# A hybrid decoder block on one core: expert keys turned by block transposes on VectorE, one equality for both gate masks, and 78 instead of 64 early blocks

## Chip, cores and metric

One Trainium2 chip, one of its cores. The metric is the device time in microseconds (us) of one execution. Lower is better.

## What is computed

One layer: adaLN conditioning, sliding-window attention and a gated delta rule in parallel, a gated mix of the two with an output projection, then a PEER channel mixer. 512 tokens, width 1024, everything in float32. The change is in the output projection, in PEER and in what connects them:

```
mix = (sigmoid(gate_a) * y_a + sigmoid(gate_b) * y_b) @ w_out
x = x + gate1 * mix
h2 = rms_norm(x, norm2_gain) * (1.0 + scale2) + shift2
x = x + gate2 * peer(h2, peer_w_q, peer_sub_keys, peer_u, peer_v)

# peer: 8 heads, 2 x 128 sub-keys, top 16 of 16 x 16 pairs -> 128 of 16384 experts a token
hid = gelu(einsum('td,ted->te', xb, u_tab[ib]))
out = einsum('te,ted->td', hid * gb, v_tab[ib])
```

## The kernel before, in words

The phases up to the delta rule are not touched. `phase_mix` streams weight slabs of 256 columns (1 MB): SyncE (SP) loads a slab, ScalarE (ACT) rounds it to a high part (`split_hi`, L394), VectorE (DVE) takes the rest as a low part (`split_lo`, L398), TensorE (PE) multiplies three products. Slabs 12 to 15 are w_out, 16 to 23 the PEER queries. At L1446 one DMA brings x back as `x2T`.

`phase_peer` does not gather experts for most tokens. The 128 tokens of the first tile are done with gathers (two of 512 KB for each of 128 slots, issued by GpSimd, L1919 and L1948; `dot` L2348 and `add` L2363 on DVE). For the other 384 tokens it goes densely through all 16384 experts, in 128 blocks of 128 experts. For each block b:

- SP loads `u_raw` (128 experts x 1024, 512 KB, L1850). PE turns it by 8 transposes of 128x128 into PSUM (L1974 early, L1964 late). ACT makes the high part (L2128, L2120) and, early, a float32 copy for GpSimd (L2131). The low part comes from GpSimd early (`low`, L1926, two operations of 128x512) and from DVE late (`u_lo`, L2343).
- PE makes the hidden products: 24 matmuls of 384 columns (L1994 and L2000 early, L2080 to L2082 late); ACT applies gelu.
- Later the block is weighted by its gates (`weights`, DVE L2377), split (`w_hi` ACT L2233, `w_rest` DVE L2381) and multiplied with the block of v, itself split (`v_hi` ACT L2217, `v_rest` DVE L2367): `mixed(n)`, 18 matmuls of 512 columns (L2096).

The hidden products of NA = 64 blocks are made early, while DVE selects experts, and kept in DRAM. The work has three stages, and the order on each engine is written out by hand:

- **Stage S** (selection). DVE runs `tile(t)` four times: top 16 by max, find and replace, the pairs, and comparisons and folds in bfloat16. PE meanwhile does the steps `ahead(i)` for i below SIDE = 400, ten steps a block, so 40 early blocks.
- **Stage G** (gates). The gates of 384 tokens become dense tables by one-hot products, in 96 groups of 4 tokens. For each group DVE writes the masks `hot_i` (one comparison of 128x512, L2333) and `hot_j` (four `tensor_scalar` of 128x128 that compare and scale by the gate, L2338), PE multiplies them (L2064), ACT moves the result out (L2199), and every 8 groups SP stores 2 MB. Four buffers of masks let DVE be four groups ahead. PE does 22 more early blocks between groups and two after the last (TAIL).
- **Stage C** (combination). For n = 0 to 127 the loop does `mixed(n - 1)` and, at odd n ("fused"), the late turn and `hidden` of one of the 64 late blocks; even n ("known") read theirs back from DRAM. On DVE an iteration is `v_rest(n)`, `dot(n + 4)`, `weights(n)`, `add(n)`, `w_rest(n)`. `v_hi(n)` on ACT waits for the end of `mixed(n - 2)` (semaphore `yp`), since v and w have two buffers each.

The end is 16 vector operations and 8 stores.

## Time and profile before

| | |
|---|---|
| median of 3 runs | 2312.81 us (2312.73, 2312.81, 2315.75) |
| profiled execution, span | 2314.9 us |
| PE / PE weight loads | 2231.1 us (96%) / 1952.0 us (84%) |
| DVE / ACT / GpSimd (POOL) | 1680.0 (73%) / 910.7 (39%) / 714.2 us (31%) |
| DMA | 442.36 MB, mean 191 GB/s |

The profile is of one execution; what is worked out from its rows is set against its own span. "Busy" is the time in which an engine had an instruction in it, waiting for a port included. A row of the timeline can merge several instructions of a line (x4); its duration is then theirs together. Durations of neighbours overlap a little, so the distance from start to start (the pitch) is what an instruction costs its engine in a row of others.

### The profile page before, as it was taken

The numbers are of one execution on the slowest core, as the hardware profiler recorded it, in microseconds if no ns is written. First come the engines' busy times: TensorE is split into PE (matmuls) and PEld (weight loads), VectorE is DVE, ScalarE is ACT, GpSimd is POOL, SyncE is SP. The second block draws the span as 40 slices with busy tenths as digits, with TensorE's granted clock in tenths as the row PEclk, the third lists the DMA queues.
The fourth block names the chain that finished last, engine by engine and source line by source line (L and its number), as shares of the span: only waits on it lengthen the run. The fifth ranks groups of instructions, "written<-read, shape, count | busy, mean of one in ns | idle before, by whom it ended". The sixth has DMA issues, their size and how long they took to land.

```text
span 2314.9 us, 35852 instructions
## 1 busy us (share of the span) xinstructions
PE 2231.1 (96%) x14109; PEld 1952.0 (84%) x14109; DVE 1680.0 (73%) x3265; ACT 910.7 (39%) x1592; POOL 714.2 (31%) x646
## 2 busy tenths in 40 slices
...
GB/s 292 88 103 111 119 128 46 29 29 33 46 53 109 86 125 81 91 120 135 130 143 165 191 219 295 362 325 324 316 322 320 317 324 321 315 345 323 315 326 119
DMA packets 224998, 442.36 MB, mean 191 GB/s; under 512 B 22423, under 2 KB 138304, under 8 KB 224576
## 3 DMA queue, kind: packets, MB, share of 16 engines
...
## 4 chain that ended last, share of the span: by engine, by line
PE 46%; DVE 8%; ACT 1%; DMA 1%; issue 0%; SPq 0%; POOL 0%; ACTq 0%; POOLq 0%
PE bank L2096 22%; DVE hot_j L2338 5%; PE bank L1994 5%; PE bank L2082 4%; PE bank L2080 4%; PE bank L2081 4%; PE bank L2000 2%; PE bank L1964 2%; DVE hot_i L2333 2%; PE bank L1974 2%; PE bank L2016 1%; DMA u_raw<-in_peer_u_dram 1%; PE bank L2064 1%; DMA ug<-in_peer_u_dram,gidx 0%; DVE o_nat L2419 0%
## 5 line engine op out<-in xcount | busy, mean ns | idle before, releaser
L1926 POOL TENSOR_TENSOR ua_lo<-ua,ua_hi 128x512 fp32r<-128x512 f32 x128 | 193.9, 1533 | 389.1 <-ACT ua L2131 388.8
L1919 POOL DMA_INDIRECT ug<-in_peer_u_dram,gidx x128 | 146.1, 1142 | 335.1 <-DVE ug L2348 332.1
L2096 PE MATMUL bank<-vt_hi,wg_hi 128*128 128x512 f32 x768 | 246.2, 402 | 0.7 <-DVE wg_lo L2381 0.7
L2096 PE MATMUL bank<-vt_lo,wg_hi 128*128 128x512 f32 x768 | 237.8, 391 | 0.0
L2096 PE MATMUL bank<-vt_hi,wg_lo 128*128 128x512 f32 x768 | 237.5, 390 | 0.0
L2367 DVE TENSOR_TENSOR vt_lo<-vt_raw,vt_hi 128x1024 fp32r<-128x1024 f32 x128 | 156.4, 1222 | 101.5 <-ACT vt_hi L2217 101.5
L1948 POOL DMA_INDIRECT vg<-in_peer_v_dram,gidx x128 | 130.0, 1015 | 226.9 <-DVE g_acc L2363 217.2
L1994 PE MATMUL bank<-h_hi,ua_hi 128*128 128x384 f32 x512 | 177.4, 346 | 1.9 <-ACT ha L2144 1.9
L2080 PE MATMUL bank<-h_hi,uT_hi 128*128 128x384 f32 x512 | 177.6, 347 | 0.0
L2217 ACT ACTIVATE vt_hi<-vt_raw 128x1024 fp32r<-128x1024 f32 x128 | 135.1, 1055 | 96.7 <-PE bank L2096 95.2
L2233 ACT ACTIVATE wg_hi<-wt 128x384 fp32r<-128x384 f32 x127 | 66.9, 526 | 269.3 <-DVE wt L2377 269.3
L1994 PE MATMUL bank<-h_lo,ua_hi 128*128 128x384 f32 x512 | 172.8, 337 | 0.0
L2082 PE MATMUL bank<-h_hi,uT_lo 128*128 128x384 f32 x512 | 172.5, 337 | 0.0
L2081 PE MATMUL bank<-h_lo,uT_hi 128*128 128x384 f32 x512 | 171.9, 336 | 0.0
L2096 PEld LDWEIGHTS bank<-vt_lo,wg_hi 128*128 128x128 f32 x768 | 144.2, 188 | 31.4
L2096 PEld LDWEIGHTS bank<-vt_hi,wg_lo 128*128 128x128 f32 x768 | 144.2, 188 | 31.4
L2096 PEld LDWEIGHTS bank<-vt_hi,wg_hi 128*128 128x128 f32 x768 | 134.7, 188 | 34.3 <-issue 13.6
L2363 DVE SCALAR_TENSOR_TENSOR g_acc<-vg,g_hw,g_acc 128x1024 f32<-128x1024 f32 x127 | 162.5, 1280 | 1.1
L2348 DVE SCALAR_TENSOR_TENSOR ug<-ug,h2n 128x1024 f32<-128x1024 f32 x128 | 157.1, 1228 | 3.5 <-DMA ug<-in_peer_u_dram,gidx 3.5
L2120 ACT ACTIVATE uT_hi<-bank 128x512 fp32r<-128x512 f32 x128 | 75.5, 589 | 191.3 <-PE bank L1964 183.5
L2338 DVE TENSOR_SCALAR hot_j<-iota,picked,picked 128x128 f32<-128x128 f32 x384 | 150.0, 450 | 0.0
L2343 DVE TENSOR_TENSOR uT_lo<-bank,uT_hi 128x512 fp32r<-128x512 f32 x128 | 88.2, 689 | 67.3 <-ACT uT_hi L2120 65.0
...
## 6 DMA issues: line engine op xcount, KB each, us to landing
u_raw<-in_peer_u_dram SPq DMA_DIRECT2D x128, 512.0 KB
vt_raw<-in_peer_v_dram SPq DMA_DIRECT2D x128, 512.0 KB
...
```

The costliest lines, as they stand in the source:

```text
L1919: nc.gpsimd.indirect_dma_start(ug[s % RING][:], None, u_rows, bass.IndirectOffsetOnAxis(m.gidx[:, s:s + 1].bitcast(U32), 0)).then_inc(s_ug ...
L1926: nc.gpsimd.tensor_tensor(ua_lo[b % 2][:, 4 * q:4 * q + 4, :], ua[b % 2][:, 4 * q:4 * q + 4, :], ua_hi[b % 2][:, 4 * q:4 * q + 4, :].bitca ...
L1994: last = pe.matmul(o, ua_hi[b % 2][:, k, :], (m.h2_lo if low else m.h2_hi)[:, k, P:], start=(n == 0), stop=False)
L2080: pe.matmul(o, uT_hi[f % 2][:, k, :], m.h2_hi[:, k, P:], start=(k == 0), stop=False)
L2081: pe.matmul(o, uT_hi[f % 2][:, k, :], m.h2_lo[:, k, P:], start=False, stop=False)
L2082: last = pe.matmul(o, uT_lo[f % 2][:, k, :], m.h2_hi[:, k, P:], start=False, stop=(k == KC - 1))
L2096: ins = pe.matmul(y_bank[t][q][:], w[n % 2][:, tok], v[n % 2][:, 512 * q:512 * q + 512], start=(first and i == 0), stop=(last and i == 2))
L2217: nc.scalar.activation(v_hi[n % 2][:], v_raw[n % 4][:], ACT.Copy).then_inc(x["vhi"], 1)
L2338: ins = v.tensor_scalar(B[n % 4][:, t, :], m.iota[:], jT[:, col], gT[:, col], ALU.is_equal, ALU.mult)
L2348: v.scalar_tensor_tensor(ug[s % RING][:], ug[s % RING][:], 1.0, m.h2n[:], ALU.mult, ALU.mult, accum_out=h_raw[:, s:s + 1]).then_inc(x["dot ...
L2363: ins = v.scalar_tensor_tensor(acc[:], vg[s % RING][:], h_w[:, s:s + 1], acc[:], ALU.mult, ALU.add)
L2367: v.tensor_tensor(v_lo[n % 2][:], v_raw[n % 4][:], v_hi[n % 2][:].bitcast(F32), ALU.subtract)\
```

## The change

u is laid out so that DVE can turn it. VectorE's `transpose` turns each 32x32 square by itself, so channels are dealt in another order: SP loads `u_raw` by four DMAs of 32 partitions (rows of 1 KB), and whatever meets u follows that order: the columns of w_out (four pieces of 64 columns, rows of 256 bytes), the rows of the query weights (four DMAs of 32 partitions), x2T (eight DMAs of 32 partitions), h2n, the scale, shift and gate columns (`dealt`, 16 small DMAs from GpSimd at the start of the mix), and the evacuations that write through a rearranged view.

The 8 transposes a block leave PE. DVE does one `transpose` of 128x1024 a block: in stage S wherever `spent` has counted 13 units of selection work (195 units a tile, so 60 blocks over four tiles), then 8 blocks after the first group (b = 60 to 67) and one every 8 groups; in stage C `turn_late(f + 1)` opens each fused iteration. ACT makes only the high part, from SBUF. All low parts are GpSimd's, also the late ones (`u_lo`).

The masks: one comparison of 128x1024 on DVE writes both, and the gate is multiplied in afterwards, by two ACT operations of 128x128 and one GpSimd operation of 128x256 (`scale`). NA is 78, SIDE is 512 steps of eight a block (64 blocks), then 12 blocks between the groups and two after. The gathers of the first four slots are issued after the groups. In stage C there are 50 fused iterations among 128, two or three apart. Two PSUM banks take turns for the hidden products.

```diff
-NA = 64
+NA = 78
...
+def load_rows(self, sp, pair, u, pieces):
+    sp.wait_ge(self.lo_done, pair * 2 + (u - 1))
+    for dst, src in pieces:
+        sp.dma_start(self.raw[u][dst, :, :], src).then_inc(self.loaded[u], 16)
...
+if dealt:
+    for half in range(SLAB_BLOCKS):
+        raw, hi, _ = self.halves(u, half)
+        last = self.m.nc.scalar.activation(hi, raw, ACT.Copy)
+    last.then_inc(self.hi_done, 1)
+    return
...
+for s in range(D // SLAB):
+    slabs.append([(slice(64 * i, 64 * i + 64), w_o[:, :, QD * i + 64 * s:QD * i + 64 * s + 64]) for i in range(4)])
+for s in range(2 * D // SLAB):
+    slabs.append([(slice(QB * i, QB * i + QB), w_q[i, :, :, SLAB * s:SLAB * s + SLAB]) for i in range(4)])
...
-    sp.dma_start(m.x2T[:].rearrange("p k n -> p (k n)"), m.xT_dram).then_inc(z["xt"], 16)
-st.load(sp, s // 2, s % 2, False, [(slice(0, SLAB), slabs[s])])
+    for i in range(4):
+        for h in range(2):
+            sp.dma_start(m.x2T[QB * i:QB * i + QB, 4 * h:4 * h + 4, :], x_rows[:, 2 * i + h])\
...
+for i in range(4):
+    for l in range(4):
+        src = m.mod[QB * l:QB * l + QB, 16:40].rearrange("p (v k) -> p v k", k=KC)[:, :, 2 * i:2 * i + 2]
+        nc.gpsimd.dma_start(m.dealt[QB * i:QB * i + QB, l, :, :], src).then_inc(z["deal"], 16)
+pool.wait_ge(z["deal"], 16 * 16)
...
-STEPS = 10 * NA
-GROUPS = TD // GT
-TAIL = 20
-TURNS = (0, 1)
-SIDE = 400
-SCORES = {82: 2, 184: 3}
-EXPS = {92: 0, 194: 1, 292: 2}
-PICKS = {270: 1, SIDE: 2}
+PARTS = 8
+STEPS = PARTS * NA
+TAIL = 16
+SIDE = 512
+SCORES = {105: 2, 235: 3}
+EXPS = {118: 0, 248: 1, 374: 2}
+PICKS = {346: 1, SIDE: 2}
 LATE = 24
+SCALED = 2
...
-known = [n % 2 == 0 and n < 2 * NA for n in range(NB)]
-fused = [n for n in range(NB) if not known[n]]
-NF = len(fused)
-at = [fused.index(n) if not known[n] else n // 2 for n in range(NB)]
+NF = NB - NA
+fused = [n for n in range(NB) if (n + 1) * NF // NB > n * NF // NB]
+knowns = [n for n in range(NB) if n not in fused]
+known = [n in knowns for n in range(NB)]
+at = [knowns.index(n) if known[n] else fused.index(n) for n in range(NB)]
...
-    sp.wait_ge(z["turn"], 2 * (b - 2))
-sp.dma_start(u_raw[b % 3][:], u_dram[:, n, :]).then_inc(s_u[b % 3], 16)
+    sp.wait_ge(z["turn"], b - 2)
+for i in range(4):
+    rows = u_raw[b % 3][QB * i:QB * i + QB, :].rearrange("b (c w) -> b c w", c=4)
+    src = u_dram[:, n, QD * i:QD * i + QD].rearrange("(c b) w -> b c w", b=QB)
+    sp.dma_start(rows, src).then_inc(s_u[b % 3], 16)
...
+def low(b):
+    pool.wait_ge(z["uev"], b + 1)
+    if b >= 2:
         pool.wait_ge(z["hid"], b - 1)
-    nc.gpsimd.tensor_tensor(ua_lo[b % 2][:, 4 * q:4 * q + 4, :], ua[b % 2][:, 4 * q:4 * q + 4, :],
-                            ua_hi[b % 2][:, 4 * q:4 * q + 4, :].bitcast(F32), ALU.subtract).then_inc(z["ulo"], 1)
-low(0, 0)
-low(0, 1)
-for b in range(NA):
-    if b + 1 < NA:
-        low(b + 1, 0)
-        low(b + 1, 1)
+    for q in range(2):
+        nc.gpsimd.tensor_tensor(blocks(ua_lo[b % 2], q), turned(ua[b % 3], q),
+                                blocks(ua_hi[b % 2], q).bitcast(F32), ALU.subtract).then_inc(z["ulo"], 1)
+def u_lo(f):
+    pool.wait_ge(x["uhi"], f + 1)
+    for q in range(2):
+        nc.gpsimd.tensor_tensor(blocks(uT_lo[f % 2], q), turned(uT, q),
+                                blocks(uT_hi[f % 2], q).bitcast(F32), ALU.subtract).then_inc(x["ulo"], 1)
...
+def scale(n):
+    pool.wait_ge(z["eq"], n + 1)
+    tok = slice(GT * n + SCALED, GT * n + GT)
+    half = hot[n % 4][:, 1, SCALED:GT, :]
+    nc.gpsimd.tensor_tensor(half, half, share[:, tok].rearrange("p (t o) -> p t o", o=1)
+                            .to_broadcast([P, GT - SCALED, P]), ALU.mult).then_inc(z["pab"], 1)
...
+low(0)
+for i in range(SIDE):
+    ahead(i)
+scale(0)
+scale(1)
+for n in range(GROUPS):
+    if n + 2 < GROUPS:
+        scale(n + 2)
+    for i in side(n):
+        ahead(i)
+for s in range(RING):
+    gather_u(s)
+for i in range(STEPS - TAIL, STEPS):
+    ahead(i)
+keep(NA - 1)
 pool.wait_ge(z["pte"], NT - 1)
-for s in range(RING, SLOTS + AHEAD):
+for s in range(RING, NB + 2 * RING):
...
+n = s - 2 * RING
+if s == RING + 2:
+    u_lo(0)
+if n >= 0 and not known[n] and at[n] + 1 < NF:
+    u_lo(at[n] + 1)
...
+b, j = divmod(i, PARTS)
+o = bank[6 + b % 2][:, 0:TD]
+for n in range(3 * j, 3 * j + 3):
     if n == 0:
-        pe.wait_ge(z["uev"], 2 * b + 2)
-        if b:
-            pe.wait_ge(z["gelu"], b)
+        pe.wait_ge(z["uev"], b + 1)
+        if b >= 2:
+            pe.wait_ge(z["gelu"], b - 1)
...
+pe.wait_ge(z["pab"], n + 1)
...
+def u_hi(f):
+    act.wait_ge(x["ut"], f + 1)
+    if f >= 2:
         act.wait_ge(x["h"], f - 1)
-    nc.scalar.activation(uT_hi[f % 2][:, 4 * q:4 * q + 4, :], t_bank[:].rearrange("p (k n) -> p k n", k=4),
-                         ACT.Copy).then_inc(x["uhi"], 1)
-def evac(b, q):
-    act.wait_ge(z["turn"], 2 * b + q + 1)
-    if q == 0 and b >= 2:
+    if f == 0:
+        act.wait_ge(s_st[0], 16 * BATCHES // 2)
+    hi, src = whole(uT, uT_hi[f % 2])
+    nc.scalar.activation(hi, src, ACT.Copy).then_inc(x["uhi"], 1)
+def evac(b):
+    act.wait_ge(z["turn"], b + 1)
+    if b >= 2:
         act.wait_ge(z["hid"], b - 1)
-    src = bank[7 - 2 * q][:].rearrange("p (k n) -> p k n", k=4)
-    nc.scalar.activation(ua_hi[b % 2][:, 4 * q:4 * q + 4, :], src, ACT.Copy)
-    if b >= 2:
-        act.wait_ge(z["ulo"], 2 * b + q - 3)
-    nc.scalar.activation(ua[b % 2][:, 4 * q:4 * q + 4, :], src, ACT.Copy).then_inc(z["uev"], 1)
+    hi, src = whole(ua[b % 3], ua_hi[b % 2])
+    nc.scalar.activation(hi, src, ACT.Copy).then_inc(z["uev"], 1)
...
+def scale(n):
+    act.wait_ge(z["eq"], n + 1)
+    for t in range(SCALED):
+        col = slice(GT * n + t, GT * n + t + 1)
+        half = hot[n % 4][:, 1, t, :]
+        last = nc.scalar.activation(half, half, ACT.Copy, scale=share[:, col])
+    last.then_inc(z["ab"], 1)
...
+PACE = 13
+def turn(b):
+    r = u_raw[b % 3]
+    dve.wait_ge(s_u[b % 3], 64 * (b // 3 + 1))
+    if b == 0:
+        dve.wait_ge(z["fill"], 2 * NT + 2)
+    if b == 2:
+        dve.wait_ge(s_x2[0], 32)
+        dve.wait_ge(s_x2[1], 32)
+    if b >= 3:
+        dve.wait_ge(z["ulo"], 2 * (b - 2))
+    v.transpose(ua[b % 3][:], r[:]).then_inc(z["turn"], 1)
+    state["b"] += 1
+def spent(n):
+    state["work"] += n
+    if state["work"] >= PACE:
+        state["work"] -= PACE
+        turn(state["b"])
...
-    v.tensor_tensor(A[n % 4][:], m.iota[:].rearrange("p (o n) -> p o n", o=1).to_broadcast([P, GT, P]),
-                    iT[:, tok:tok + GT].rearrange("p (t o) -> p t o", o=1).to_broadcast([P, GT, P]),
-                    ALU.is_equal)
-    for t in range(GT):
-        col = slice(tok + t, tok + t + 1)
-        ins = v.tensor_scalar(B[n % 4][:, t, :], m.iota[:], jT[:, col], gT[:, col], ALU.is_equal, ALU.mult)
-    ins.then_inc(z["ab"], 1)
-def u_lo(f, q):
-    dve.wait_ge(x["uhi"], 2 * f + q + 1)
-    v.tensor_tensor(uT_lo[f % 2][:, 4 * q:4 * q + 4, :], t_bank[:].rearrange("p (k n) -> p k n", k=4),
-                    uT_hi[f % 2][:, 4 * q:4 * q + 4, :].bitcast(F32), ALU.subtract).then_inc(x["ulo"], 1)
+    rows = hot[n % 4][:].rearrange("p k t n -> p (k t) n")
+    v.tensor_tensor(rows, m.iota[:].rearrange("p (o n) -> p o n", o=1).to_broadcast([P, 2 * GT, P]),
+                    pair[:, n].rearrange("p k (t o) -> p (k t) o", o=1).to_broadcast([P, 2 * GT, P]),
+                    ALU.is_equal).then_inc(z["eq"], 1)
+    while state["b"] < NA and PARTS * (state["b"] - 3) <= reached(n):
+        turn(state["b"])
+def turn_late(f):
+    r = (NA + f) % 3
+    dve.wait_ge(s_u[r], 64 * ((NA + f) // 3 + 1))
+    if f:
+        dve.wait_ge(x["uhi"], f)
+        dve.wait_ge(x["ulo"], 2 * f)
+    else:
+        dve.wait_ge(z["hid"], NA - 1)
+    v.transpose(uT[:], u_raw[r][:]).then_inc(x["ut"], 1)
...
 dot(0)
 dot(1)
-u_lo(0, 0)
+turn_late(0)
 v_rest(0)
 dot(2)
-u_lo(0, 1)
+dve.wait_ge(z["ulo"], 2 * NA)
 weights(0)
 dot(3)
...
-    u_lo(f + 1, 0)
+    turn_late(f + 1)
 v_rest(n)
 if n + AHEAD < SLOTS:
     dot(n + AHEAD)
 if not known[n]:
-    if f + 1 < NF:
-        u_lo(f + 1, 1)
```

## Rows read from the trace of the kernel before

**Rows 1.** The page: busy time of the engines.
```profile
PE 2231.1 (96%) x14109; PEld 1952.0 (84%) x14109; DVE 1680.0 (73%) x3265; ACT 910.7 (39%) x1592; POOL 714.2 (31%) x646
```
**Rows 2.** The chain that ended last, in order of time: start, us, what.
```profile
1026.41 2.81 PE bank L1994 x16
...
1031.49 2.81 PE bank L1994 x16
...
1232.60 1.79 PE bank L2064 x16
...
1461.70 4.34 PE bank L2096 x18
...
1484.42 8.25 PE bank L2096 x36
...
1497.73 8.28 PE bank L2096 x36
```
**Rows 3.** The chain again, end of the early blocks.
```profile
1436.72 1.40 PE bank L2000 x8
```
**Rows 4.** Timeline of DVE, the ends of stage S.
```profile
1009.91 3.19 DVE L2243 MAX8 tv<-scores 128x8 f32<-128x128 f32 x16 [9.51 <-ACT scores L2151]
...
1216.84 0.69 DVE L2333 TENSOR_TENSOR hot_i<-iota,picked 128x512 f32<-128x512 f32 x1
```
**Rows 5.** Timeline of GpSimd, stage G.
```profile
1299.97 3.19 POOL L1926 TENSOR_TENSOR ua_lo<-ua,ua_hi 128x512 fp32r<-128x512 f32 x2 [0.27 <-ACT ua L2131]
```
**Rows 6.** Timeline of DVE over the same us.
```profile
1300.11 0.68 DVE L2333 TENSOR_TENSOR hot_i<-iota,picked 128x512 f32<-128x512 f32 x1
1300.71 3.06 DVE L2338 TENSOR_SCALAR hot_j<-iota,picked,picked 128x128 f32<-128x128 f32 x4
1303.68 0.68 DVE L2333 TENSOR_TENSOR hot_i<-iota,picked 128x512 f32<-128x512 f32 x1
1304.29 1.10 DVE L2338 TENSOR_SCALAR hot_j<-iota,picked,picked 128x128 f32<-128x128 f32 x4
1305.31 0.68 DVE L2333 TENSOR_TENSOR hot_i<-iota,picked 128x512 f32<-128x512 f32 x1
```
**Rows 7.** Lines, shapes apart: busy us, mean ns of one, idle before.
```profile
L1926 POOL TENSOR_TENSOR ua_lo<-ua,ua_hi 128x512 fp32r<-128x512 f32 x128 | 193.9, 1533 | 389.1 <-ACT ua L2131 388.8
...
L540 POOL TENSOR_TENSOR ada_w<-ada_w,silu_c 128x1024 f32<-128x1024 f32 x32 | 63.1, 1971 | 8.6 <-DMA ada_w<-in_w_ada_dram 8.0
```
**Rows 8.** Timeline of DVE where the first two dots run.
```profile
1429.12 1.21 DVE L2348 SCALAR_TENSOR_TENSOR ug<-ug,h2n 128x1024 f32<-128x1024 f32 x1
1430.27 0.08 DVE L2348 DVE_READ_ACCUMULATOR ug<-ug,h2n 128x1 f32 x1
1430.27 2.30 DVE L2348 SCALAR_TENSOR_TENSOR ug<-ug,h2n 128x1024 f32<-128x1024 f32 x1
```
**Rows 9.** Timeline of one known iteration of stage C.
```profile
1701.46 0.67 PE L2096 MATMUL bank<-vt_hi,wg_hi 128*128 128x512 f32 x2
1701.73 1.06 ACT L2217 ACTIVATE vt_hi<-vt_raw 128x1024 fp32r<-128x1024 f32 x1 [1.54 <-PE bank L2096]
...
1702.82 1.23 DVE L2367 TENSOR_TENSOR vt_lo<-vt_raw,vt_hi 128x1024 fp32r<-128x1024 f32 x1 [1.53 <-ACT vt_hi L2217]
...
1703.96 1.22 DVE L2348 SCALAR_TENSOR_TENSOR ug<-ug,h2n 128x1024 f32<-128x1024 f32 x1
...
1705.11 0.85 DVE L2377 TENSOR_TENSOR wt<-hl,gate 128x384 f32<-128x384 f32 x1
...
1705.87 1.28 DVE L2363 SCALAR_TENSOR_TENSOR g_acc<-vg,g_hw,g_acc 128x1024 f32<-128x1024 f32 x1
...
1707.07 0.55 DVE L2381 TENSOR_TENSOR wg_lo<-wt,wg_hi 128x384 fp32r<-128x384 f32 x1
```
**Rows 10.** DVE, one-input float32 operation of 128x1024.
```profile
1454.86 0.75 DVE L2360 TENSOR_SCALAR g_acc<-vg,g_hw 128x1024 f32<-128x1024 f32 x1
```
**Rows 11.** Windows: us, busy by engine, granted clock, DMA share, GB/s.
```profile
1290.00:1400.00 110.00, 109.78 (x820) 109.22 (x819) 110.00 (x263) 62.00 (x118) 42.73 (x38) 1.00 0.62 200
...
1700.00:1800.00 100.00, 100.00 (x510) 87.11 (x509) 81.19 (x109) 34.04 (x57) 32.00 (x30) 1.00 0.90 318
...
2070.00:2080.00 10.00, 9.03 (x42) 7.04 (x40) 7.68 (x11) 3.09 (x5) 3.25 (x3) 1.00 1.02 420
```

More of the change, by code:

```diff
@@ L42 @@
 TD = SEQ - P
-NA = 64
+NA = 78
 FIRST = 3
+QD = D // 4
+QB = P // 4
 EARLY_FILL = 12
@@ L387, in load, with halves, split_hi @@
             sp.dma_start(self.raw[u][:, :, dst], src).then_inc(self.loaded[u], 16)
-    def split_hi(self, act, u, s, loads, first):
+    def load_rows(self, sp, pair, u, pieces):
+        sp.wait_ge(self.lo_done, pair * 2 + (u - 1))
+        for dst, src in pieces:
+            sp.dma_start(self.raw[u][dst, :, :], src).then_inc(self.loaded[u], 16)
+    def halves(self, u, half):
+        raw = self.raw[u][:].rearrange("p k (i h a) -> p h k i a", h=SLAB_BLOCKS, a=QB)[:, half]
+        hi, lo = (w[u][:, :, P * half:P * half + P].rearrange("p k (i a) -> p k i a", a=QB) for w in (self.hi, self.lo))
+        return raw, hi, lo
+    def split_hi(self, act, u, s, loads, first, dealt=False):
         act.wait_ge(self.loaded[u], loads)
@@ L393, in split_hi, with split_lo @@
             act.wait_ge(self.ready, s * 2 - 2)
+        if dealt:
[4 more added lines that the diff above has]
+            return
         self.m.nc.scalar.activation(self.hi[u][:], self.raw[u][:], ACT.Copy).then_inc(self.hi_done, 1)
-    def split_lo(self, dve, u, s):
+    def split_lo(self, dve, u, s, dealt=False):
         dve.wait_ge(self.hi_done, s + 1)
+        if dealt:
+            for half in range(SLAB_BLOCKS):
+                raw, hi, lo = self.halves(u, half)
+                last = self.m.nc.vector.tensor_tensor(lo, raw, hi.bitcast(F32), ALU.subtract)
+            last.then_inc(self.lo_done, 1)
+            return
         self.m.nc.vector.tensor_tensor(self.lo[u][:], self.raw[u][:], self.hi[u][:].bitcast(F32),
@@ L1429, in phase_mix @@
     GATES, A, B, OUT, WQ, N = (0, 5, 6, 7), 1, 8, 12, 16, 24
-    z = {n: m.sem("mix_" + n) for n in "sig rest rest_sig ahi alo ohi olo xt mixed mhi mlo x2 x2a sq ms msr sqrt ht h hh split2 os om oe or on".split()}
+    z = {n: m.sem("mix_" + n) for n in "deal sig rest rest_sig ahi alo ohi olo xt mixed mhi mlo x2 x2a sq ms msr sqrt ht h hh split2 os om oe or on".split()}
     bank = m.bank
@@ L1750, in phase_peer @@
     pick = [m.at(f"pick{i}", [P, 3, PH * TOPK], 170 + 1.5 * i) for i in range(2)]
-    picked = [m.at(f"picked{k}", [P, TD], 192 + 2 * k) for k in range(3)]
+    GT = 4
+    GROUPS = TD // GT
+    pair = m.at("picked_pair", [P, GROUPS, 2, GT], 192)
+    share = m.at("picked_gate", [P, TD], 195)
     m.h2n = m.at("h2n", [P, D], 202)
@@ L1934, in _, with keep, ahead @@
+            def keep(b):
                 pool.wait_ge(z["gelu"], b + 1)
                 nc.gpsimd.dma_start(m.hid_dram[b, :, :], hst[b % 2][:]).then_inc(s_h[b % 2], 16)
-                if b == NA - 5:
-                    pool.wait_ge(z["ab"], 1)
-                    for s in range(RING):
-                        gather_u(s)
-            pool.wait_ge(z["pte"], NT - 1)
-            for s in range(RING, SLOTS + AHEAD):
+            def ahead(i):
+                b, j = divmod(i, PARTS)
+                if j == 0 and b + 1 < NA:
+                    low(b + 1)
+                if j == 2 and b:
+                    keep(b - 1)
```

210 lines of the change are left out of this document (100 added, 110 removed).

## The prediction

> **What bounds the kernel now.** I read the page first: PE is busy 96% of the span, DVE 73% [rows 1]. That average hides three stages, so I went on to the chain of waits in order of time, for their borders. Stage S runs until the first group at 1232.60, stage G until the last early block ends at 1436.72 + 1.40 = 1438.1, stage C from there to the end [rows 2, 3]. In S an early block takes 5.08 us (1031.49 - 1026.41), of which 2.81 + 1.39 = 4.20 are its 24 products and the rest its transposes [rows 2, 3]. In C a known and a fused iteration take 13.31 us together (1497.73 - 1484.42), 8.28 of them two `mixed` [rows 2]. But DVE is nearly full too: selection runs without a break from 1009.91 to 1216.84 [rows 4], and in G it is busy 110.00 of 110 us, in C 81.19 of 100 [rows 11]. So the reader is to see two engines at their limit in S and G, and one, with slack on DVE, in C.
>
> The timeline shows what fills DVE in G. A group costs it 1.63 us (1303.68 to 1305.31) when alone. While GpSimd makes a low part, four `hot_j` take 3.06 us instead of 1.10 [rows 5, 6]. So a DVE operation that reads two tensors in SBUF, or `hot_j`, and a GpSimd operation shut each other out, for 3.06 - 1.10 = 1.96 us a block. A `dot` was caught in the same way, 2.30 us after 1.21 [rows 8]. In C GpSimd now only issues gathers, and nothing of the kind shows.
>
> **Stage S.** PE loses the transposes, DVE gains 60 of 128x1024. No row has that operation. A one-input float32 operation of that size took 0.75 us [rows 10], a two-input one has a pitch of 1.14 (1702.82 to 1703.96) [rows 9], and twice that, 2.28, is my upper end. I take 1.14, the pitch of most float32 operations of that width in the trace, and keep 0.75 and 2.28 for the range. The Trainium skill (Vector Engine (DVE) Microarchitecture Reference, 3.8) says that the transposing front end sustains one element per cycle and lane; at the 0.96 GHz that the skill's Trainium Kernel Development and Optimization (NeuronCore Architecture) gives VectorE, 1024 elements would be an estimate of 1.07 us, and the sum would be 4 us lower in this stage. No run here shows it yet.
>
> DVE: 206.9 us of selection [rows 4] + 60 x 1.14 = 68.4 + 3 until the first u has landed (0 to 6) + 5 for more blocks' low parts in the way (0 to 15) = 283.3, so selection ends at 1293.2. A turn comes each 206.9 / 60 + 1.14 = 4.59 us, slower than PE's 4.20: DVE sets this stage. Blocks 60 to 63 are turned only after it: comparison 1.14, turn 1.14, high part 1.06 [rows 9], then 4 x 4.20 = 16.8 on PE. First group at 1313.3, **80.7 us later** than now. What should have paid for it, 24 early blocks more without transposes, is PE's time, not DVE's.
>
> **Stage G.** One comparison of 1024 columns, 1.14 (the pitch of such an operation), takes the place of 1.63. But GpSimd now multiplies 128x256 in every group and reads SBUF for it, so by rows 5 and 6 it and the comparison alternate. Its price: 1.97 us for 1024 columns is 0.49 for 256, 1.53 for 512 is 0.77 [rows 7]; I take 0.60. Low parts: 1.96 / 8 = 0.25 a group, for 12 blocks instead of 22. Ten turns, 0.12 a group, read one tensor, so half may lie beside GpSimd: 0.06. Sum 2.05. PE needs 1.79 / 2 + 4.20 / 8 = 1.42 [rows 2, 3], ACT, busy 62.00 of 110 us here [rows 11], loses a copy and gets two operations of 128x128, some 1.5 us a group; both are covered. 95 x 2.05 + 2 x 4.20 = 203.2 against 205.5: **2.3 us less**. Bounds a group: 1.87 (0.49, turns hidden) to 2.28 (0.77, turns paid), so -17 to +22 us. A 2 MB store still stands in SP's queue ahead of each u load; DVE's four buffers cover some 8 us of it, and I price the rest at nothing (0 to 15 us).
>
> **Stage C.** Now 2314.9 - 1438.1 = 876.8. PE loses 14 hidden blocks of 4.20 = 58.8, and 64 turns of 13.31 - 8.28 - 4.20 = 0.83, 53.1. That would leave 765. Two things take some back. First, two known iterations in a row. `mixed(m)` needs `w_rest(m)`, and that chain starts when `mixed(m-2)` ends: from 1701.46, where PE goes on, over v_hi, v_rest, dot, weights and add to the end of w_rest at 1707.07 + 0.55, plus 0.05 to PE, it is 6.21 us [rows 9]. Today `hidden` always lies between; after a fused iteration followed by two known ones only one `mixed` of 4.14 does, so PE waits 2.07. Gaps of three between fused iterations: 3a + 2b = 128 with a + b = 50 gives 28, **58 us**. Second, the late low parts are GpSimd's: two operations beside DVE operations that read two tensors [rows 8]. In a fused iteration, from the start of `hidden`: v_hi until 1.36, v_rest until 2.50, low part, dot until 4.85, low part until 6.05, weights, add, w_rest until 8.55; PE needs that at 4.17 + 4.14 = 8.31. With hand-overs I take 0.46 x 50 = **23 us** (0, all hidden, to 50 x 1.96 = 98). The turn itself stands ahead of v_rest, under v_hi. At the start nothing late is needed for `mixed(0)`, -5 us (0 to -15). Sum 765 + 58 + 23 - 5 = 841, **36 us less**.
>
> DMA: an iteration brings 0.52 (v) + 0.39 x 0.52 (u) + 1.05 (gathers) + 0.20 (gate) + 0.61 x 0.20 = 2.09 MB, over 841 / 128 = 6.6 us 318 GB/s, what it is now; the queues have moved 420 [rows 11]. The u loads of 32 partitions have no row: at the same rate they cost nothing, at half the rate the equivalent is 2.30 MB, 350 GB/s, still under 420; 0 to 15 us. The Trainium skill (SBUF — State Buffer, Door 1: The DMA port swizzle) would halve them, since 32 partitions reach 8 of the 16 ports; by that the sum is in the upper part of these 15 us. No row here shows it.
>
> **Mix.** x2T by eight DMAs and w_out in short rows arrive later; both have slack of some us, and split halves add about 0.2 us each. I take +1 (0 to 6). The 16 `deal` DMAs run on an idle GpSimd. If that cover went, each would cost about what a GpSimd issue costs, 1 us.
>
> **Sum.** 80.7 - 2.3 - 36 + 1 = +43 on the span of 2314.9. The span lies 2.1 above the median of the runs, so I forecast 2312.8 + 43 = **2356 us**, slower.
>
> **Rivals.** (a) Faster: the comparison reads broadcast operands, and it may leave GpSimd its port. Then a group costs max(1.42, 1.14 + 0.12, 1.5) = 1.5, 95 x 0.55 = 52 us less, and if the late low parts hide too, another 23: 2281. It decides once the exclusion saves more than the 43. For it: `hot_i` mostly took 0.68. Against: at 1299.97 GpSimd's pair took 3.19 and let `hot_i` end first [rows 5, 6]. Chance 0.13. (b) Turns at 2.28: 60 x 1.14 = 68 more in S, 10 x 1.14 = 11 in G, and in C 50 x 0.8 = 40, where they no longer fit under v_hi: 2475. Chance 0.08. (c) GpSimd reads its u through runs of 32 elements; 1.5 times slower low parts, or half-rate u loads, add 12 in G and 25 in C: 2393. Chance 0.14. (d) Both ends of S and G low together (turns 0.75, no waits): -23 - 8 - 17 and a shorter start of C, -10: 2298 to 2315, where it is no change or slightly faster. Chance 0.05. The change not doing what it says would show as PE still turning u in C; nothing speaks for it.
>
> **Numbers.** Forecast 0.60, own range 2330 to 2385. Low end 2290 takes in (d) but not all of (a), high end 2410 takes in (c) but not (b); that leaves out some 0.2. A difference of 0.2%, 4.6 us, is about what this kernel's runs can tell from none. Faster: (a) and part of (d), 0.15; same 0.03; slower 0.82.
>
> **What would show it.** Right: `transpose` near 1.2 us; first group near 1313; groups every 2.0 to 2.1 us with DVE comparisons of 1.2 and some of 1.8; PE in C waiting for `w_rest` some 1.5 to 2 us in 28 places, and late low parts longer than 1.3. Wrong: DVE idle in G, which is rival (a); or no wait of PE between known iterations, when C would take 765 and the whole 2280.

## The result, and the profile after

The median is 2430.13 us (four runs, 2418.72 to 2436.38) against 2314.28 us before (four runs on the same chip), a ratio of 1.0493 with an interval of 1.0469 to 1.0517: slower by 4.9%. The sign of the forecast (2356 us) was right, its size was not: the result lies above the range.

The page of the changed kernel (time of the profiled execution 2418.72 us), in answer to [rows 1], with the 40 slices of granted clock and DMA share:

```profile
span 2416.9 us, 34092 instructions
...
PE 2167.7 (90%) x13085; PEld 1869.5 (77%) x13085; DVE 1772.7 (73%) x2885; ACT 902.4 (37%) x1532; POOL 1104.2 (46%) x900
...
PEclk9999998999999999999999899899999999898999
DMA  8333331101132354355555567998999989888894
```

PE has 63 us less work than before and is idle more; GpSimd has 390 us more. The borders of the stages come from PE's timeline: its first product of a group, and the last eight of the last early block (first the kernel before, then the changed one):

```profile
1441.66 1.55 PE L2000 MATMUL bank<-h_hi,ua_lo 128*128 128x384 f32 x8
```
```profile
1506.27 1.55 PE L2071 MATMUL bank<-h_hi,ua_lo 128*128 128x384 f32 x8
```

The first row corrects the forecast's reading: the last early block ended at 1443.2, not at 1438.1. [Rows 3] are the block before it. From the last early block to the end is stage C. In the table "first group" is a time from the start of the span, G and C are lengths; "late u", "order" and "low" are explained below.

| kernel | first group | G | C | median us | ratio to before |
|---|---|---|---|---|---|
| before | 1232.4 | 210.8 | 871.7 | 2314.28 | |
| changed | 1303.0 | 204.8 | 909.1 | 2430.13 | 1.0493 [1.0469, 1.0517] |
| forecast of it | 1313.3 | 203.2 | 841 | 2356 | |
| e1 late u in one DMA | 1309.8 | 209.5 | 879.5 | 2389.64 | 1.0326 [1.0293, 1.0359] |
| e2 late u ahead | 1304.0 | 207.7 | 841.0 | 2354.63 | 1.0189 [1.0156, 1.0222] |
| e3 no late low | 1307.0 | 204.9 | 882.3 | 2393.64 | 1.0347 [1.0318, 1.0377] |
| e4 order | 1307.8 | 205.9 | 856.0 | 2377.68 | 1.0294 [1.0261, 1.0328] |
| e5 = e2 + e4 | 1309.4 | 207.4 | 814.8 | 2326.09 | 1.0052 [1.0035, 1.0069] |
| e6 = e2 + e3 | 1298.8 | 207.8 | 840.0 | 2351.46 | 1.0174 [1.0144, 1.0205] |
| e7 = e5, low on DVE | 1312.2 | 207.4 | 797.7 | 2317.56 | 1.0018 [0.9992, 1.0043] |
| e8 = e5, three scaled on ACT | 1298.7 | 200.8 | 812.0 | 2317.06 | 1.0016 [1.0002, 1.0030] |
| e9 = e7, late u in one DMA | 1303.7 | 207.4 | 780.1 | 2291.97 | 0.9910 [0.9887, 0.9933] |
| e10 = e7, three scaled, 58 blocks | 1278.7 | 263.2 | 803.4 | 2346.70 | 1.0142 [1.0124, 1.0160] |
| e11 = e7, GpSimd scales nothing | 1309.0 | 184.5 | 787.5 | 2288.67 | 0.9904 [0.9876, 0.9933] |
| e12 = e10 with 50 + 14 blocks | 1261.2 | 201.5 | 852.2 | 2316.73 | 1.0010 [0.9993, 1.0027] |
| e13 = e10, stores later | 1276.3 | 223.0 | 796.1 | 2303.08 | 0.9962 [0.9943, 0.9981] |
| e14 = e5, no late low | 1307.4 | 208.3 | 807.0 | 2315.98 | 0.9986 [0.9968, 1.0004] |

Stage times are of one execution each. That of the changed kernel is its fastest, 11 us under its median; those of e5 and e14 are their slowest, 7 and 8 us above. Stage C is the same code in e7, e10, e11 and e13 and took 787.5 to 803.4 us, so a difference there under some 10 us says nothing by itself. The first group depends on when selection begins: at 1009.9 before and, with the same code up to there in the changed kernel and e1 to e14, anywhere from 1001.5 to 1012.0. Counted from the start of selection it comes after 222.5 us before, 297.4 in the changed kernel and 296.9 to 300.9 in the others with 64 blocks ahead of it, 274.1 and 274.4 in e10 and e13, and 255.4 in e12.

The span grew by 102.0 us: 70.6 until the first group, -6.0 in G, +37.4 in C. The forecast was off by -10, +2 and +68. So C is where to look. DVE's lines, shapes apart, from 1525 to 2395 (busy us, mean ns of one, idle before them):

```profile
L2477 DVE SCALAR_TENSOR_TENSOR g_acc<-vg,g_hw,g_acc 128x1024 f32<-128x1024 f32 x125 | 192.6, 1541 | 1.1
...
L2481 DVE TENSOR_TENSOR vt_lo<-vt_raw,vt_hi 128x1024 fp32r<-128x1024 f32 x126 | 152.1, 1207 | 58.5 <-ACT vt_hi L2294 58.3
L2491 DVE TENSOR_TENSOR wt<-hid,gate 128x384 f32<-128x384 f32 x49 | 82.5, 1683 | 14.8 <-ACT hid L2307 13.9
...
L2491 DVE TENSOR_TENSOR wt<-hl,gate 128x384 f32<-128x384 f32 x77 | 64.6, 839 | 0.0
L2458 DVE STREAM_TRANSPOSE uT<-u_raw 128x1024 f32<-128x1024 f32 x49 | 60.7, 1239 | 50.0 <-DMA u_raw<-in_peer_u_dram 50.0
```

Two things here were not in the forecast at this size. The turn waits 50.0 us for its u block. And `weights` takes 1.68 us in fused iterations and 0.84 in known ones, `add` 1.54 on average after 1.28 in [rows 9]: they stand beside GpSimd's low parts. Who waited for whom in the same stretch (us in total, times, longest):

```profile
PE bank L2166 <- DVE wg_lo L2495: 111.1, 61, 10.2
...
DVE uT L2458 <- DMA u_raw<-in_peer_u_dram: 50.0, 13, 10.1
```

PE waits 61 times for `w_rest`, not 28 times, and up to 10.2 us, not 2.07. The chain in order of time shows how a long wait comes about:

```profile
1616.63 0.50 ACT hid L2307
1617.16 1.77 DVE wt L2491
1618.94 0.33 SPq L1958
1619.31 0.43 SPq L1918
...
1620.74 8.27 DMA u_raw<-in_peer_u_dram
1629.03 1.25 DVE uT L2458
1630.28 1.10 DVE vt_lo L2481
```

`weights` frees a gate buffer; SP, which has waited for it, issues the gate load and then four u loads; they land 8.27 us after the last was issued; only then can DVE turn, and everything behind the turn in DVE's order comes late. SP puts the load of a late block in the iteration in which that block is multiplied, and SP's waits for `wt` and `vlo` hold it about four iterations ahead of DVE. The turn, though, stands one fused iteration earlier. With fused iterations two apart (22 of the 49 gaps) that leaves two iterations, with three apart (27) only one. DVE's timeline bears this out: all 13 waits for u are at turns with a gap of three to the iteration that uses the block, none is at one with a gap of two.

### The profile page after: what moved, and what is told of

Same layout as the page of the kernel before. It is cut to its first block, busy times and chain, and to the rows that moved or that the text cites. A ratio compares the mean times of both kernels' runs of the same rounds, so it can differ in the third digit from the quotient of the medians.

```text
span 2416.9 us, 34092 instructions
## 1 busy us (share of the span) xinstructions
PE 2167.7 (90%) x13085; PEld 1869.5 (77%) x13085; DVE 1772.7 (73%) x2885; ACT 902.4 (37%) x1532; POOL 1104.2 (46%) x900
## 4 chain that ended last, share of the span: by engine, by line
PE 26%; DVE 17%; DMA 6%; issue 5%; ACT 3%; POOL 2%; SPq 1%; DVEq 0%; ACTq 0%
PE bank L2166 10%; DMA u_raw<-in_peer_u_dram 5%; PE bank L2065 5%; DVE g_acc L2477 3%; PE bank L2071 3%; DVE wt L2491 3%; PE bank L2134 3%; DVE hot L2444 2%; DVE ug L2462 2%; PE bank L2152 2%; PE bank L2150 2%; PE bank L2151 2%; POOL ua_lo L1995 2%; DVE vt_lo L2481 1%; ACT vt_hi L2294 1%
## 5 line engine op out<-in xcount | busy, mean ns | idle before, releaser
L1995 POOL TENSOR_TENSOR ua_lo<-ua,ua_hi 128x512 fp32r<-128x512 f32 x156 | 231.2, 1501 | 384.6 <-ACT ua_hi L2194 384.3
L2001 POOL TENSOR_TENSOR uT_lo<-uT,uT_hi 128x512 fp32r<-128x512 f32 x100 | 196.4, 1984 | 130.8 <-ACT uT_hi L2187 130.8
L2065 PE MATMUL bank<-h_hi,ua_hi 128*128 128x384 f32 x624 | 216.3, 347 | 5.6 <-ACT ua_hi L2194 5.6
L2065 PE MATMUL bank<-h_lo,ua_hi 128*128 128x384 f32 x624 | 212.3, 340 | 0.0
L2477 DVE SCALAR_TENSOR_TENSOR g_acc<-vg,g_hw,g_acc 128x1024 f32<-128x1024 f32 x127 | 195.2, 1537 | 1.1
L2444 DVE TENSOR_TENSOR hot<-iota,picked_pair 128x1024 f32<-128x1024 f32 x96 | 151.5, 1622 | 29.1 <-PE bank L2134 28.7
L2134 PE MATMUL bank<-hot 128*128 128x128 f32 x768 | 108.0, 299 | 41.0 <-issue 38.3
L2134 PEld LDWEIGHTS bank<-hot 128*128 128x128 f32 x768 | 104.1, 213 | 45.4 <-issue 42.2
L2152 PE MATMUL bank<-h_hi,uT_lo 128*128 128x384 f32 x400 | 134.3, 336 | 0.0
L2150 PE MATMUL bank<-h_hi,uT_hi 128*128 128x384 f32 x400 | 134.2, 335 | 0.0
```

What stands on the lines that cost most here:

```text
L1995: nc.gpsimd.tensor_tensor(blocks(ua_lo[b % 2], q), turned(ua[b % 3], q), blocks(ua_hi[b % 2], q).bitcast(F32), ALU.subtract).then_inc(z["u ...
L2001: nc.gpsimd.tensor_tensor(blocks(uT_lo[f % 2], q), turned(uT, q), blocks(uT_hi[f % 2], q).bitcast(F32), ALU.subtract).then_inc(x["ulo"], 1)
L2065: last = pe.matmul(o, ua_hi[b % 2][:, k, :], (m.h2_lo if low else m.h2_hi)[:, k, P:], start=(n == 0), stop=False)
L2134: last = pe.matmul(bank[n % 4][:, P * t:P * t + P], hot[n % 4][:, 0, t, :], hot[n % 4][:, 1, t, :], start=True, stop=True)
L2150: pe.matmul(o, uT_hi[f % 2][:, k, :], m.h2_hi[:, k, P:], start=(k == 0), stop=False)
L2152: last = pe.matmul(o, uT_lo[f % 2][:, k, :], m.h2_hi[:, k, P:], start=False, stop=(k == KC - 1))
```

## Experiments

Each changes the changed kernel, or the one named. The ratios are in the table.

**e1: late u in one DMA**

```diff
+if b >= NA:
+    sp.dma_start(u_raw[b % 3][:], u_dram[:, n, :]).then_inc(s_u[b % 3], 16)
+    return
```


> The changed kernel, but the late u blocks come by one DMA of 128 partitions instead of four of 32 partitions in rows of 1 KB; their channels are then not in the dealt order, so the hidden products of the 50 late blocks are of another order of channels (same work, other numbers). Theory L1, the form of the load is what makes it late in stage C: VectorE's 50 us of waiting for u_raw (13 times, up to 10.1 us) fall under 10 and the time by 30 to 50 us, to 2380 to 2400. Theory L2, the load is issued too late (only one iteration before its use where fused iterations are three apart): waits stay above 35 us and the time within 15 us of 2430. Theory L3, the queues are full: the same as L2.

1.0326 where the changed kernel has 1.0493: less by 1.7% of the time before, some 39 us (the percentages below are meant in the same way). DVE's waits for u fell from 50.0 to 19.4 us: between the two theories by the waits, as L1 by the time. The form matters, but it isn't all: with the place in the queue unchanged, 19.4 us of waiting are left.

**e2: late u ahead.** The load moves to the iteration after the fused one before it.

```diff
+if n and not known[n - 1] and 3 <= at[n - 1] + 1 < NF:
+    load(NA + at[n - 1] + 1)
...
-elif f >= 3:
-    load(NA + f)
```


> The changed kernel, but SP issues each late u load in the iteration right after the fused one before it, so always three iterations ahead of its turn instead of one or two; nothing is left out. Theory L2 (issued too late): the waits of VectorE for u_raw, 50 us, vanish, and the time falls by 30 to 50 us, to 2380 to 2400. Theory L1 (form) or L3 (queues full): the waits only move, to the v loads or the gathers, and the time stays within 15 us of 2430.

1.0189, 3.0% less; stage C is 68 us shorter, 841.0. The cause is L2's, the gain more than it gave. No wait for u is left in DVE's lines from 1525 to 2340 (idle before it, last column):

```profile
L2458 DVE STREAM_TRANSPOSE uT<-u_raw 128x1024 f32<-128x1024 f32 x49 | 60.6, 1238 | 0.0
```

So the loads were late for their place in SP's queue; that they also came slowly made it worse (e1). Windows of the changed kernel and of e2 (us, busy by engine, clock, DMA share, GB/s):

```profile
1600.00:2200.00 600.00, 515.23 (x2331) 433.58 (x2329) 510.74 (x567) 184.94 (x259) 346.96 (x238) 0.96 0.92 302
```
```profile
1600.00:2200.00 600.00, 552.02 (x2563) 464.53 (x2561) 553.60 (x624) 206.02 (x285) 383.69 (x261) 1.00 0.99 332
```

One move gave back 10% more matmuls in the same 600 us (2563 against 2331), and the granted clock went from 0.96 to 1.00, while PE's longest wait for `w_rest` went from 10.2 to 1.6 us.

**e3: no late low**

```diff
+if f >= 2:
+    nc.gpsimd.engine_nop().then_inc(x["ulo"], 2)
+    return
```


> The changed kernel, but GpSimd makes the low part only of the first two of the 50 late blocks and only signals for the other 48 (the low parts of these blocks are left out; the products use old ones). Theory X1, exclusion between GpSimd and VectorE is the mis-sized term in stage C, priced at 23 us where VectorE's own durations have grown by some 90 us: add goes from 1.54 back to 1.28 us, the weights of fused iterations from 1.68 to 0.84, and the time falls by 60 to 100 us, to 2330 to 2370. Theory X2, the price of 23 us was right and the rest is late loads and other waits: the time falls by 15 to 30 us.

1.0347, 1.5% less, some 34 us: nearer X2. DVE's durations went back as X1 said (`add` 1.28, fused `weights` 0.86), but the waits for u grew to 71.5 us and took part of it.

**e4: order.** Known iterations: weights, v_rest, w_rest, dot, add.

```diff
+if known[n]:
+    weights(n)
 v_rest(n)
+if known[n]:
+    w_rest(n)
...
```


> The changed kernel, but in a known iteration VectorE does weights, v_rest and w_rest before dot and add, instead of after; nothing is left out. The chain from the end of one mixed to the start of the next but one is then about 3.1 us instead of 6.2, under the 4.14 of one mixed. Theory K1, the waits of TensorE between known iterations are paid as forecast (28 times 2.07, 58 us, and the lower granted clock behind them): the time falls by 50 to 80 us, to 2350 to 2380. Theory K2, they lie beside waits that are there anyway (late u, exclusion): it falls by less than 25 us.

1.0294, 2.0% or some 46 us less, and 53 us less in stage C: 2378, as K1. But the waits for u also fell, from 50.0 to 33.1, so the two are mixed here.

**e5: both**


> The kernel with the u loads issued three iterations ahead, and besides that VectorE does weights, v_rest and w_rest before dot and add in known iterations; nothing is left out. With the loads alone stage C took 841.0 us (2352.7 - 1511.7) and the time was 2354.6. Theory K1, what is left of the waits between known iterations is still paid: TensorE's 75 waits for w_rest, 76.7 us, fall under 30 and the time falls by 40 to 60 us more, to 2295 to 2315. Theory K2, the two repairs mend the same waits (the weights first gained 53 us of stage C alone, partly by giving late loads room): under 20 us more, 2335 to 2355.

Stage C 814.8, 26 us under e2 (28 by the medians): between K1 and K2. From 1540 to 2290 PE waits for `w_rest` 41.0 us in 46 places, after 59.9 in 71 in e2; K1 wanted under 30. The 76.7 us in its text hold one wait of 14.6 at the start of the stage.

**e6: loads ahead, no late low**


> The kernel with the u loads issued three iterations ahead, and besides that without the late low parts on GpSimd from the third late block on (48 of 50 are left out, the products use old ones); VectorE's order as in the change. Theory X3, the late low parts cost what was forecast, 23 us, once the loads are in time: stage C falls from 841 to 810 to 825. Theory X1, exclusion is dearer, by VectorE's own durations some 70 to 90 us: stage C falls to 750 to 780. Theory X0, they lie under TensorE: within 8 us of 841.

Stage C 840.0: X0. The waits of PE for `w_rest` from 1540 to 2290, first in e2 and then in e6:

```profile
PE bank L2166 <- DVE wg_lo L2495: 59.9, 71, 1.6
```
```profile
PE bank L2169 <- DVE wg_lo L2498: 53.0, 27, 2.2
```

What is left in e6 is the forecast's chain alone: 1.96 us a place here, and over the whole stage, without a wait of 14.1 at its start, 55.4 us in 29 places, where the forecast had 28 of 2.07, 58 us. The low parts added many short waits, but only 6.9 us in sum. And hardly that was won (1.0 us in C, 3 by the medians). Windows of e6, which answer to e2's above:

```profile
1600.00:2200.00 600.00, 556.92 (x2560) 476.46 (x2559) 493.54 (x624) 201.77 (x284) 212.71 (x189) 0.97 0.98 332
```

About the same number of matmuls in the same 600 us, but PE is busy 5 us more for them, at a granted clock of 0.97 instead of 1.00. So what was won in waiting was given back in slower products. Fewer and longer waits (up to 2.2 us instead of 1.6) went with some time at the lower of the clock's two levels; that they are the reason was not tried apart.

**e7: order, loads ahead, low on DVE**

```diff
-if n >= 0 and not known[n] and at[n] + 1 < NF:
-    u_lo(at[n] + 1)
...
+def u_lo(f):
+    dve.wait_ge(x["uhi"], f + 1)
+    ...
+    v.tensor_tensor(lo, src, hi.bitcast(F32), ALU.subtract).then_inc(x["ulo"], 2)
```


> As the kernel with loads ahead and weights first, but VectorE makes the late low parts itself (one subtraction of 128x1024 a block after dot in a fused iteration) and GpSimd only issues gathers; nothing is left out. By VectorE's durations in the change the low parts on GpSimd lengthen add by 0.26 in all iterations and the fused weights by 0.84; the subtraction costs 1.14. Theory X1: 0.26 x 128 + 0.84 x 50 + 11 = 86 us of VectorE go and 57 come, and as VectorE is not the bound in every iteration the time is 5 to 30 us under the kernel with GpSimd's low parts. Theory X4, what counts is the chain within a fused iteration, which gets 1.14 longer: 0 to 40 us slower than it.

797.7 in C, 17 us under e5, and 8.5 us by the medians. That is X1's size, but the intervals of the two ratios overlap, so it is likely and not shown. The two-input subtraction that DVE now makes itself takes 1.22 us; GpSimd's two took 1.98 each. Then look at the last columns (e7 from 1600 to 2200):

```profile
1600.00:2200.00 600.00, 574.87 (x2700) 493.86 (x2699) 558.50 (x692) 215.16 (x299) 317.73 (x198) 0.99 1.03 346
```

A share of 1.03: the queues are full. They nearly were in e2 (0.99 at 332 GB/s) and were in e5 (1.02 at 344). I then asked whether they set the stage.

**e8: three of four masks scaled by ACT** (`SCALED = 3`, on e5)


> As the kernel with loads ahead and weights first, but in stage G ScalarE scales three of the four masks of a group and GpSimd one (128x128 instead of 128x256); nothing is left out. In the change stage G is 204.8 us, 2.13 a group. Theory G1, VectorE and GpSimd take turns at the port and set the stage: GpSimd's 0.60 becomes some 0.35, and stage G is 20 to 25 us shorter. Theory G2, ScalarE becomes the bound: 3 x 0.35 + 0.55 + 0.2 = 1.8 a group, stage G 10 us shorter at most or unchanged. Theory G3, the stage hangs on handing four buffers round between four engines: unchanged within 5 us.

G is 6.6 us shorter than e5's, and 4 under the shortest of the kernels in which GpSimd scales two masks (204.8 to 209.5); the time is 8 to 9 us less. G2's size.

**e9: e7 with late u in one DMA** (e1's edit)


> As the kernel with loads ahead, weights first and late low parts on VectorE, but the late u blocks come by one DMA of 128 rows of 4 KB instead of four DMAs in rows of 1 KB (their channels are then not in the dealt order: same work, other numbers). The kernel it is compared with took 797.7 us in stage C (2317.3 - 1519.6) with its DMA queues at a share of 1.03 and 346 GB/s from 1600 to 2200. Theory D1, the queues now bound stage C and short rows cost them time: the share falls under 1.0 and the stage by 12 to 35 us. Theory D2, TensorE and the chain of VectorE bound it: within 8 us.

0.9910 against e7's 1.0018, 1.1% less, with intervals apart; C is 17.6 us shorter. The queues, per us, move more at a smaller share:

```profile
1600.00:2200.00 600.00, 588.36 (x2779) 506.63 (x2778) 574.38 (x714) 222.68 (x308) 346.04 (x203) 1.00 0.96 358
```

With the u loads in rows of 1 KB the queues were full (1.03) at 346 GB/s, in rows of 4 KB 358 left room (0.96). As D1: the queues held stage C back, and the short rows cost.

**e10: 58 blocks before the first group, and e8's edit** (`SIDE = 464`, on e7)


> As the kernel with loads ahead, weights first and late low parts on VectorE, but ScalarE scales three masks of a group, and TensorE does 58 instead of 64 early blocks before the first group and 18 instead of 12 between the groups; nothing is left out. In the change selection ended near 1276 and the last 7 turns waited for TensorE, the first group came at 1303.0. Theory S1, the blocks before the first group are what stage S waits for: the first group comes 20 to 27 us earlier, six more low parts in stage G cost 12 us (1.96 each), GpSimd's shorter scaling gives back some 7, and the time is 12 to 25 us under that kernel, 2292 to 2305. Theory S2, VectorE sets stage S as forecast: the first group moves less than 8 us, and the time is 0 to 8 us over or under.

Counted from the start of selection, the first group came after 274.1 us instead of some 297: 23 us earlier, as S1. (e7 itself needed 300.9 and began selection 6.6 us later, so by the table it is 33.5.) But stage G is 56 us longer, as neither. In G, DVE waited in this way (from 1290 to 1530):

```profile
DVE ua L2320 <- DMA u_raw<-in_peer_u_dram: 76.6, 10, 13.5
```

and SP's own timeline has a u load right behind a store:

```profile
1297.85 0.38 SPq L1927 DMA_DIRECT2D gates<-g_stage  x1
1298.28 9.59 SPq L1918 DMA_DIRECT2D u_raw<-in_peer_u_dram  x8
```

A store waits for eight groups, and the u block behind it in the queue is needed to get to them. With 18 instead of 12 blocks between the groups the store stands too early.

**e13: the same, each store of gates one u load later**

```diff
-while k < BATCHES and reached(Q * (k + 1)) <= PARTS * (b - 4) + 4:
+while k < BATCHES and reached(Q * (k + 1)) <= PARTS * (b - 5) + 4:
```


> As the kernel with 58 blocks before the first group (2346.7 us; first group 1278.7, but VectorE then waited 73 us for u blocks in stage G, each behind a store of gates in SP's queue), but each store of gates stands one u load later in SP's queue; nothing is left out. Theory S1 with the store as the reason: the first group stays near 1279, the waits for u in stage G fall from 73 to under 10 us, stage G goes from 263 back to 200 to 215, stage C stays at some 798 to 805, and the time comes to 2285 to 2305, under the kernel before the change (2315). Theory S3, the queues are too full for u loads in stage G whatever their order: waits over 40 us, time over 2325.

G 223.0 (missed by 8; DVE waits 20.9 us for GpSimd's low parts), no wait for u left in it, and 2303.08 us, inside S1's range. 0.9962 [0.9943, 0.9981]: of the kernels that leave nothing out and keep the order of channels, this one alone is under the kernel before, by 0.4%.

**e11: GpSimd scales nothing** (on e7)

```diff
-nc.gpsimd.tensor_tensor(half, half, share[:, tok] ... , ALU.mult).then_inc(z["pab"], 1)
+nc.gpsimd.engine_nop().then_inc(z["pab"], 1)
```


> As the kernel with loads ahead, weights first and late low parts on VectorE, but GpSimd doesn't multiply by the gate in stage G, it only signals (two of four tokens keep an unscaled mask; that multiplication is left out). Stage G was 207.4 us, 2.16 a group. Theory G1, the comparison and GpSimd's operation alternate at the port (0.60 a group was forecast): stage G falls by 35 to 60 us. Theory G3, the stage hangs on the hand-over of four buffers between VectorE, ScalarE, TensorE and back, or on ScalarE: it falls by less than 15 us.

G 22.9 us shorter, 184.5: between the theories. The comparison still takes 1.40 us on average, beside low parts, and the group 1.92. So GpSimd's multiplication is worth 0.24 a group here, not 0.60. What holds the group at 1.92, over 1.40 for the comparison and 0.13 for turns, wasn't tried; DVE waits 26.8 us for PE to free a buffer. (0.9904 is of a kernel with work left out, so it is no gain.)

**e12: 64 early blocks, 50 before the first group** (on e10, with a turn every 15 units)


> As the kernel with 58 blocks before the first group, but with 64 early blocks in all as before the change: 50 before the first group, 12 between the groups, 2 after, and every second iteration of stage C fused; a turn every 15 units of selection instead of 13. Nothing is left out. Theory N1, early blocks pay: the first group comes 25 to 35 us earlier, but stage C has 14 more late blocks, each 4.20 of TensorE and 1.24 + 1.22 of VectorE, and grows by 40 to 60 us: 10 to 30 us slower than the kernel with 78. Theory N2, TensorE has room in stage C beside the queues: stage C grows by 15 to 30 us, and the time is 0 to 15 us under it.

The first group came at 1261.2, and C took 852.2, 49 to 65 us more than the same schedule with 50 late blocks: N1 for stage C. But the first group, 51 us earlier than e7's, nearly paid for that, so the whole is 2316.73 us, no slower than e7 or e8 with 78. Against e13, which has 78 blocks and three scaled masks too, and no store in the way of its u loads, it is 0.5% slower, 11 us, with intervals apart: the low end of N1's 10 to 30. So the 14 blocks that the change moved from late to early are worth something between nothing and 11 us.

**e14: e5 without late low parts**


> As the kernel with loads ahead and weights first (stage C 814.8 us), but without the late low parts on GpSimd from the third late block on (48 of 50 left out, the products use old ones). In VectorE's old order leaving them out took TensorE's waits from 76.7 to 53.3 us and gained nothing (841.0 to 840.0), while the granted clock from 1600 to 2200 was 0.97 instead of 1.00. Theory X5, the low parts on GpSimd cost what VectorE's wait chain lets through, some 20 to 40 us now that the other chain is mended: stage C 775 to 795. Theory X6, the queues set stage C at some 798, as with low parts on VectorE: 795 to 805, with TensorE waiting less and the queues' share at 1.03.

C 807.0, 8 us under e5 (15 by the ratios) and no better than with the low parts on DVE (797.7, and ratios that overlap): nearer X6. (The 76.7 and 53.3 us in its text are of stretches that begin differently; over the same one they are 59.9 and 53.0, as above.) The share from 1600 to 2200 is 1.03, and DVE waits for u again, though each load is three iterations ahead:

```profile
DVE uT L2461 <- DMA u_raw<-in_peer_u_dram: 49.1, 22, 10.1
```

## Why the forecast was right, and where it failed

**What failed: stage C's DMA term, "0 to 15 us", and with it the place of the late loads.** C was to take 841 and took 909.1. With the loads three iterations ahead, and nothing else changed, it took 841.0. So the 68 us are the late u loads (70 by the ratios). I counted bytes and rates, and the bytes were fine; what I didn't do is take the load, its line in SP's queue, and the turn that needs it, and count the iterations between them in the new pattern of two and three. The step "the turn itself stands ahead of v_rest, under v_hi" took the data as there. It cost more than DVE's 50.0 us of waiting. PE's granted clock was 0.96 with these stops and 1.00 without them; how much of the other 18 us that is was not taken apart.

**The queue's limit.** "Still under 420" was read from a window of 10 us in [rows 11]. Over 600 us the queues are full (1.03) at 346 GB/s in e7, at 333 in e12 and 354 in e11, all with u in rows of 1 KB, and no window of this length that I read moved more than 358. The forecast's own 350 GB/s, its equivalent for u loads at half the rate, is already at that limit. The form of the load has a price too: one DMA of 128 partitions took some 39 us off the changed kernel, where the loads were late besides, and 25 off e7, more than the forecast's 15. The Trainium skill (SBUF — State Buffer, Door 1: The DMA port swizzle) says that 32 partitions reach half of the ports; the runs agree in sign, but the length of the rows was changed along with the partitions, so which of the two it is stays open.

**Known-known chain, 58 us: right as a wait.** 55.4 us in 29 places in e6. Its worth in time is less sure: the order that shortens it took 26 us off stage C (e5), where the queues were full by then. **Low parts, 23 us: too much, with the loads in time.** Then they added 6.9 us of waiting and 1.0 to the stage. Beside late loads they cost 27 us of stage C (e3), in e5's order 8 (e14). DVE's own durations had grown far more, by 0.26 x 125 + 0.84 x 49 = 74 us, and in e2 most of it lay in slack. **Start, -5: wrong.** `mixed(0)` begins 15.6 us after the last early block, 13.5 before the change, since the load of the gates has to wait for their last store; the chain after the last early block:

```profile
1499.12 13.55 DMA gates<-g_stage
1512.75 6.18 DMA gate<-gates
...
1519.05 2.63 DVE wt L2491
```

So that e2 meets the forecast's 841 to the us is partly luck: the low parts were some 20 too dear, the start 7 too cheap, and the border of [rows 3], read one block early, had put 5.1 us into C that belong to G. With these three put right the forecast would be some 823, so about 18 us of e2's stage have no term in the sum, and no run here shows what they are. The loads are the one term whose error is of the size of the miss.

**Stage G: 203.2 forecast, 204.8 measured**, but not by the forecast's terms: it had 0.60 a group for GpSimd's scaling, and taking that away gave 0.24 (e11). The comparison's exclusion is real: it takes 1.18 us at 1399.75 and 2.20 at 1272.66, 1.62 on average, and 1.40 with nothing to scale on GpSimd (e11). The sum was right and its parts weren't, so its closeness is luck. PE was no longer near its limit there, and its clock fell (windows of the changed kernel, in answer to [rows 11], where G had 109.78 us of 110 at 1.00):

```profile
1310.00:1400.00 90.00, 71.73 (x484) 69.70 (x483) 75.58 (x53) 59.72 (x150) 71.21 (x63) 0.90 0.53 160
1400.00:1490.00 90.00, 73.04 (x508) 71.31 (x507) 75.76 (x50) 59.08 (x149) 67.65 (x60) 0.92 0.65 198
```

**Stage S: 80.7 forecast, 70.6 measured.** Of the 10 us between them 4.3 are only that selection began earlier (1005.6, not 1009.9). The price of a turn, 1.14, was the right end: a turn is busy for 1.24 us. By the Trainium skill (Vector Engine (DVE) Microarchitecture Reference, 3.8), which has one element per cycle and lane, the estimate was 1.07; the trace is 0.17 us above it. But the limit was named wrongly. DVE was through with selection at 1272.66 instead of 1293.2, and then waited for PE's 64th block (the ends of stage S on DVE):

```profile
1272.66 2.20 DVE L2444 TENSOR_TENSOR hot<-iota,picked_pair 128x1024 f32<-128x1024 f32 x1
1274.78 1.23 DVE L2330 STREAM_TRANSPOSE ua<-u_raw 128x1024 f32<-128x1024 f32 x1
...
1285.32 1.25 DVE L2330 STREAM_TRANSPOSE ua<-u_raw 128x1024 f32<-128x1024 f32 x1 [2.32 <-POOL ua_lo L1995]
1288.89 1.25 DVE L2330 STREAM_TRANSPOSE ua<-u_raw 128x1024 f32<-128x1024 f32 x1 [2.32 <-POOL ua_lo L1995]
```

Selection itself took 267.1 us with 61 turns (75.3 us) in it and 5.6 of waiting, so 186.2 without them, where [rows 4] gave 206.9. So selection without its turns was 20 us shorter than before; why, wasn't tried. "DVE sets this stage" held until 1272.66, PE set the last 30 us, and six blocks fewer moved the first group by 23 us (e10, e13), close to the 25 that they cost PE.

**The store in SP's queue, priced at nothing:** right for this change, where no wait for u showed in G, and only just: six blocks more and it cost 56 us (e10). **Rivals.** (a) fell: DVE and GpSimd do exclude each other. (b) fell: 1.24. (c) had late low parts and slow u loads in it; the low parts took 1.98, the u loads were late, and by its 25 us in C it was still much too small. It was the right place to look. (d) needed turns of 0.75 and no waits, and fell with (b)'s number.
